# A feed-forward's falling product by Strassen's seven products of quadrants

## What is computed

```python
h2 = rms_norm(x, g_pre_ffn) * (1.0 + sc2) + sh2              # 2048 x 1024, float32
gate, up = jnp.split(h2 @ w_gate_up, 2, axis=-1)             # w_gate_up 1024 x 5632
f = (jax.nn.silu(gate) * up) @ w_down                        # w_down 2816 x 1024
x = x + gt2 * rms_norm(f, g_post_ffn)
```

## Time and profile before

| what | us |
|---|---|
| median of three runs | 3232.58 |
| the profiled execution, its own time | 3233.96 |
| its span, first to last instruction | 3232.2 |
| feed-forward, four chunks of about 364 | 1766 to 3232 |
| in each, rising product | 243 |
| in each, falling product | 120 |

### The profile page before, as it was taken

The page is one execution under the profiler, slowest core; times in us unless marked ns, Lnnn a source line. Parts: engine busy times, 40 slices in busy tenths (PEclk is TensorE's granted clock), DMA queues, the critical chain, the costliest instruction groups (busy, mean ns, idle before and its releaser), DMA issues. The chain is left out here.

```text
span 3232.2 us, 42237 instructions
## 1 busy us (share of the span) xinstructions
PE 2889.3 (89%) x14392; PEld 2338.4 (72%) x14392; DVE 1691.8 (52%) x3092; ACT 1571.3 (49%) x3006; POOL 323.3 (10%) x1001
## 2 busy tenths in 40 slices
PE   6578888788878888689897999999999999999998
PEld 2456666666666667578786888878888788888887
DVE  2246777677868878745454444244433544254433
ACT  0457777778787786875433222232223222232222
POOL 0112222212121120110111000000000000000000
PEclk8787889899989889789998999999999999999999
DMA  5000000000000000121356333343333433343333
GB/s 212 7 24 14 24 14 14 14 14 14 14 4 14 12 27 35 66 102 63 121 175 195 93 97 96 124 144 97 95 123 107 130 97 97 122 144 97 97 98 118
DMA packets 286883, 254.86 MB, mean 79 GB/s; under 512 B 8684, under 2 KB 238616, under 8 KB 286616
## 3 DMA queue, kind: packets, MB, share of 16 engines
q1 hardware_dynamic: 282584, 236.32, 23.6%
q10 hardware_dynamic: 4160, 16.78, 1.4%
HBM read 219.50 MB, written 33.57 MB: 78 GB/s over the span
## 5 line engine op out<-in xcount | busy, mean ns | idle before, releaser
L2104 ACT ACTIVATE p_hi<-raw 128x1024 fp32r<-128x1024 f32 x264 | 279.5, 1059 | 669.4 <-PE ubank L2038 339.0
L2183 DVE TENSOR_TENSOR p_lo<-raw,p_hi 128x1024 fp32r<-128x1024 f32 x264 | 323.5, 1225 | 404.8 <-ACT p_hi L2104 404.8
L1231 ACT ACTIVATE signs<-score,pick 128x512 int8<-128x512 f32 (+6 forms) x224 | 304.8, 1361 | 42.0 <-POOL pick L743 28.5
L1209 ACT ACTIVATE logit<-tbank 128x512 f32<-128x512 f32 (+3 forms) x448 | 215.1, 487 | 211.9 <-PE tbank L962 208.8
L1381 DVE TENSOR_SCALAR_CACHE_REDUCE above<-score,cand 128x384 uint8<-128x384 f32 (+6 forms) x224 | 315.8, 1410 | 3.7
L962 PE MATMUL tbank<-ident,logit 128*128 128x128 f32 x1336 | 249.3, 300 | 69.1 <-ACT logit L1199 61.4
L978 PE MATMUL obank<-vb,logit 128*128 128x64 f32 x2176 | 298.3, 282 | 0.0
L978 PEld LDWEIGHTS obank<-vb,logit 128*128 128x128 f32 x2176 | 292.0, 207 | 0.0
L2036 PE MATMUL gbank<-x_hi,p_hi 128*128 128x512 f32 x704 | 276.5, 393 | 14.8 <-DVE p_lo L2183 14.8
L847 PE MATMUL work<-w_in,h_T 128*128 128x512 f32 (+1 forms) x768 | 283.2, 516 | 0.7 <-ACT h_T L1040 0.7
L2037 PE MATMUL gbank<-keys,p_hi 128*128 128x512 f32 x704 | 275.9, 392 | 0.0
(11 more groups left out here) (236 smaller groups left out, 5143.3 us busy)
## 6 DMA issues: line engine op xcount, KB each, us to landing
raw<-in_w_gate_up SPq DMA_DIRECT2D x176, 512.0 KB, 3.8
raw<-in_w_down SPq DMA_DIRECT2D x88, 512.0 KB, 3.7
w_in<-in_w_ada ACTq DMA_DIRECT2D x4, 4096.0 KB, 13.1
wada<-in_w_ada SPq DMA_DIRECT2D x4, 2048.0 KB, 15.5
row<-in_x SPq DMA_DIRECT2D x16, 512.0 KB, 3.9
mixT<-oT SPq DMA_DIRECT2D x32, 256.0 KB, 2.3
x_rows<-in_x SPq DMA_DIRECT2D x16, 512.0 KB, 4.7
x<-x_rows SPq DMA_DIRECT2D x16, 512.0 KB, 3.1
```

The lines of the kernel that those rows point to most:

```text
L1231: nc.scalar.activation(signs[:, 0:L], score[:, b % 2, 0:L], ACT.Sign, scale=-1.0, bias=pick[:].bitcast(F32), accum_out=less_more[:]).then_ ...
L2104: nc.scalar.activation(p_hi[:, s], raw[:, s], ACT.Copy).then_inc(panel_high, 1)
L2183: nc.vector.tensor_tensor(p_lo[:, s], raw[:, s], p_hi[:, s].bitcast(F32), ALU.subtract).then_inc(panel_ready, 1)
```

## The change

The falling product of a chunk is a product of 512 x 2816 by 2816 x 1024. Both operands are cut into four quadrants: A11 to A22 of 256 tokens by 1408, B11 to B22 of 1408 by 512. Strassen's scheme makes the four quadrants of the result from seven products M1 to M7 in place of eight, each of a sum or difference of quadrants (or a single one) on either side. Each M runs over 11 blocks of 128 rows (KQ). A **unit** is one M at one block: 2 tiles of 128 tokens by 3 matmuls of 128 x 512. There are 77 units in three groups: M1, M2, M5 side by side (units 0 to 32), then M3, M6 (33 to 54), then M4, M7 (55 to 76), each pair or triple turn by turn.

What each engine does for it:

- SyncE loads quadrant blocks of w_down (128 x 512, 256 KB each) into `quads`, four slots of up to three: two quadrants per block in the first group, three in the others. Before, each block of w_down was loaded once per chunk, 11.5 MB; now it is 88 quadrant blocks, 23 MB.
- VectorE makes b_sum (L2306, 512 columns) and a_sum (L2312, 256 columns) for unit u + 3 behind the low parts of unit u, and the low parts of each unit (L2322: 512 columns, into p_lo or b_lo; L2326: 256 columns, a_lo).
- ScalarE makes the high parts of each unit, likewise 512 and 256 columns, in six slots.
- The activations stay unsplit in `a`; the rising step's a_hi and a_lo parts go.
- The seven products are added up in `down`: ScalarE copies M2 and M5 out of their banks, VectorE combines, 16 additions of 512 columns per chunk (L2330): four at unit 35, six at unit 57, six behind the last unit. M4 uses gbank0 and ubank0, so the next rising product waits for its additions.
- The last chunk has no `last_product` any more; its squares follow the last additions.

The diff, cut to its core:

```diff
+KQ = KF // 2
+GROUPS = [("M1", "M2", "M5"), ("M3", "M6"), ("M4", "M7")]
+QUADS = [(11, 22), (12, 22, 11), (21, 11, 22)]
+B_TERMS = {"M1": (11, 22, 1), "M2": (11, None, 0), "M5": (22, None, 0), "M3": (12, 22, -1), "M6": (11, 12, 1),
+           "M4": (21, 11, -1), "M7": (21, 22, 1)}
+A_TERMS = {"M1": (11, 22, 1), "M2": (21, 22, 1), "M5": (11, 12, 1), "M3": (11, None, 0), "M6": (21, 11, -1),
+           "M4": (22, None, 0), "M7": (12, 22, -1)}
+UNITS = [(g, k, m) for g in range(3) for k in range(KQ) for m in GROUPS[g]]
+NU = len(UNITS)
+LOADS = 3 * KQ
...
+
...
-        a_hi = sb("a_hi", [P, KF, TOK], F32R)
-        a_lo = sb("a_lo", [P, KF, TOK], F32R)
+        a = sb("a", [P, KF, TOK])
+        a_hi = sb("a_hi", [P, 6, TOK // 2], F32R)
+        a_lo = sb("a_lo", [P, 6, TOK // 2], F32R)
+        b_hi = sb("b_hi", [P, 2, HALF], F32R)
+        b_lo = sb("b_lo", [P, 2, HALF], F32R)
+        quads = sb("quads", [P, LOAD_SLOTS, 3, HALF])
+        b_sum = sb("b_sum", [P, 3, HALF])
+        a_sum = sb("a_sum", [P, 3, TOK // 2])
...
+        banks = {"M1": dbank[0:2], "M2": dbank[2:4], "M5": (gbank[0], ubank[0]), "M3": (gbank[1], ubank[1]),
+                 "M6": dbank[2:4], "M4": (gbank[0], ubank[0]), "M7": dbank[0:2]}
...
+            def load_quads(c, n):
+                if n >= LOAD_SLOTS:
+                    sp.wait_ge(unit_ready, 2 * (c * NU + last_unit(n - LOAD_SLOTS) + 1))
+                elif not isinstance(c, int) or c > 0:
+                    sp.wait_ge(unit_ready, 2 * c * NU)
+                g, k = divmod(n, KQ)
+                for i, q in enumerate(QUADS[g]):
+                    at = (k + KQ * (q // 10 - 1)) * P
+                    sp.dma_start(quads[:, n % LOAD_SLOTS, i], wd[at:at + P, (q % 10 - 1) * HALF:q % 10 * HALF]
+                                 ).then_inc(quads_in[n % LOAD_SLOTS], 16)
...
+                for n in range(LOAD_SLOTS, LOADS):
+                    load_quads(c, n)
+                    if n == LOAD_SLOTS + 4 and not last:
+
+                        used(sp, c, UP - 1)
+                        load_x(c + 1)
+                    if n == LOAD_SLOTS + 8 and not last:
+                        up_pair(c + 1, 0)
...
+                if refill:
+
+                    pe.wait_ge(vector_drained, c * 16 - (4, 2)[which])
...
+            def unit_product(c, u):
+                g, k, m = UNITS[u]
...
+
...
+                    pe.wait_ge(scalar_drained, c * 4 + 4)
+                bh, bl = b_slot(u, p_hi, b_hi), b_slot(u, p_lo, b_lo)
+                for t in range(2):
+                    ah, al = a_hi[:, u % 6, t * P:(t + 1) * P], a_lo[:, u % 6, t * P:(t + 1) * P]
+                    bank = banks[m][t]
+                    nc.tensor.matmul(bank[:], ah, bh, start=(k == 0), stop=False)
+                    nc.tensor.matmul(bank[:], ah, bl, start=False, stop=False)
+                    mm = nc.tensor.matmul(bank[:], al, bh, start=False, stop=(k == KQ - 1))
+                mm.then_inc(unit_used, 1)
...
+            def unit_high_part(c, u):
+                g, k, m = UNITS[u]
+                if u >= 6:
+
+                    unit_done(act, c, u - 6)
+                elif 1 <= u <= 4:
+
+                    used(act, c, UP - 2 + (u - 1) // 2)
+                if B_TERMS[m][1] is None:
+                    quads_loaded(act, c, u)
+                else:
+                    act.wait_ge(b_summed, c * sums_before(B_TERMS, NU) + sums_before(B_TERMS, u + 1))
+                nc.scalar.activation(b_slot(u, p_hi, b_hi), b_source(u), ACT.Copy).then_inc(unit_high, 1)
+                if A_TERMS[m][1] is not None:
+                    act.wait_ge(a_summed, c * sums_before(A_TERMS, NU) + sums_before(A_TERMS, u + 1))
+                nc.scalar.activation(a_hi[:, u % 6], a_source(u), ACT.Copy).then_inc(unit_high, 1)
...
-                used(act, c, PANELS - 1)
                 for t in range(TPC):
-                    square(dbank[t][:], c, 1, t)
+                    act.wait_ge(vector_drained, c * 16 + (12, 14, 15, 16)[t])
+                    square(down[:, ORDER[t], 0:HALF], c, 1, t)
...
+                for u in range(NU):
+                    unit_high_part(c, u)
+                    if u == 35:
...
+                        act.wait_ge(vector_drained, c * 16 + 10)
+                        for t in range(TPC):
+                            square(down[:, ORDER[t], HALF:], c, 0, t)
+                    if u in (62, 65, 68, 71) and not last:
+                        x_high_part(c + 1, (u - 62) // 3)
...
+                        unit_done(act, c, (NU - 3, NU - 1)[s])
                         panel_high_part(c + 1, 0, s)
...
+            def sums(c, u):
+                g, k, m = UNITS[u]
+                if u >= 3:
+                    dve.wait_ge(unit_ready, 2 * (c * NU + u - 2))
+                first, second, sign = B_TERMS[m]
+                if second is not None:
+                    quads_loaded(dve, c, u)
+                    at = [quads[:, load_of(u) % LOAD_SLOTS, QUADS[g].index(q)] for q in (first, second)]
+                    nc.vector.tensor_tensor(b_sum[:, u % 3], at[0], at[1], ALU.add if sign > 0 else ALU.subtract
+                                            ).then_inc(b_summed, 1)
+                first, second, sign = A_TERMS[m]
+                if second is not None:
+                    if u < len(GROUPS[0]) * KQ:
+                        dve.wait_ge(act_made, c * KF + k + KQ + 3)
+                    nc.vector.tensor_tensor(a_sum[:, u % 3], a_quad(k, first), a_quad(k, second),
+                                            ALU.add if sign > 0 else ALU.subtract).then_inc(a_summed, 1)
+
+            def unit_low_part(c, u):
+                m = UNITS[u][2]
+                dve.wait_ge(unit_high, 2 * (c * NU + u + 1))
+                if B_TERMS[m][1] is None:
+                    quads_loaded(dve, c, u)
+                else:
+                    dve.wait_ge(b_summed, c * sums_before(B_TERMS, NU) + sums_before(B_TERMS, u + 1))
+                nc.vector.tensor_tensor(b_slot(u, p_lo, b_lo), b_source(u), b_slot(u, p_hi, b_hi).bitcast(F32),
+                                        ALU.subtract).then_inc(unit_ready, 1)
+                if A_TERMS[m][1] is not None:
+                    dve.wait_ge(a_summed, c * sums_before(A_TERMS, NU) + sums_before(A_TERMS, u + 1))
+                nc.vector.tensor_tensor(a_lo[:, u % 6], a_source(u), a_hi[:, u % 6].bitcast(F32), ALU.subtract
+                                        ).then_inc(unit_ready, 1)
...
+                unit_done(dve, c, UNITS.index((0, KQ - 1, "M5")))
+                for t in range(2):
+                    dve.wait_ge(scalar_drained, c * 4 + t + 1)
+                    combine(down[:, t + 2, HALF:], banks["M1"][t][:], down[:, t + 2, 0:HALF], ALU.subtract)
...
+                for at, (q, t, m) in enumerate(((12, 0, "M3"), (22, 0, "M3"), (12, 1, "M3"), (22, 1, "M3"),
+                                                (22, 0, "M6"), (22, 1, "M6")), 4):
+                    if m == "M6":
+                        dve.wait_ge(vector_drained, c * 16 + (6, 8)[t])
+                    dst = down[:, t + 2 * (q // 10 - 1), (q % 10 - 1) * HALF:q % 10 * HALF]
+                    combine(dst, dst, banks[m][t][:], ALU.add)
...
+            def drain_third(c, m):
+
+                unit_done(dve, c, UNITS.index((2, KQ - 1, m)))
+                if m == "M7":
+                    for t in range(2):
+                        dve.wait_ge(vector_drained, c * 16 + (11, 13)[t])
+                        combine(down[:, t, 0:HALF], down[:, t, 0:HALF], banks[m][t][:], ALU.add)
+                    return
+                for t in range(2):
+                    for half in range(2):
+                        dst = down[:, t + 2 * half, 0:HALF]
+                        combine(dst, dst, banks[m][t][:], ALU.add)
...
+                    for u in range(3):
+                        sums(c, u)
+                    for u in range(3):
+                        unit_low_part(c, u)
+                        sums(c, u + 3)
...
+                for u in range(3, NU):
+                    unit_low_part(c, u)
+                    if u + 3 < NU:
+                        sums(c, u + 3)
+                    if u == 35:
+                        drain_first(c, first)
+                    if u == 57:
+                        drain_second(c)
+                    if u in (62, 65, 68, 71) and not last:
+                        x_low_part(c + 1, (u - 62) // 3)
+                if last:
+                    gain_half()
+                else:
+                    low_part((c + 1) * UP, 0)
+                drain_third(c, "M4")
                 if not last:
-                    for s in range(2):
-                        low_part((c + 1) * PANELS + s, s)
+                    low_part((c + 1) * UP + 1, 1)
+                drain_third(c, "M7")
```

More of the change, by code:

```diff
@@ L1830, in _, with load_of, last_unit, loaded_count @@
                 tile(NB // 2 - 1, s, s == 0)
+KQ = KF // 2
[8 more added lines that the diff above has]
```

(22 more changed lines are left out.)

255 lines of the change are left out of this document (120 added, 135 removed).

## The result

The changed kernel takes 3336.0 us (median of four runs, 3335.4 to 3336.6), the kernel before 3233.4 on the same chip (3231.3 to 3234.4): ratio 1.032, 95% interval 1.030 to 1.034. It is 3.2% slower. The forecast was 3337 us in a range of 3300 to 3390.

The account below looks back on a forecast made before the run. TensorE bounds the kernel before; VectorE was to bound the falling product after. 3 x 23.4 + 18.8 + 4.8 (turns) + 5.3 (end) + 5 (loop) = 104 us more, giving 3337 us against the median, range 3300 to 3390.

Parts of the forecast that it names:

- VectorE's row of work: Falling product: VectorE becomes the bound, 134.0 us per chunk against 105.1 of matmuls; 4.8 us per triple, 3.7 per pair.
- the self-wait: Falling product: the first sum behind a unit's low parts waits for VectorE's own last instruction, 0.12 us per unit.
- The falling products: Stage on VectorE's clock: 144.1 us against 120.7, so +23.4 per chunk, +18.8 for the last, without x part.
- the loop: Two chunks run in the loop: rows of registers and waits between low parts, 0.03 x 154 = 5 us.
- The edges: Three turns to the next chunk: TensorE starts 1.1 us late, a stall grows 0.5; 4.8 us in all.
- The stall before step 1: Next rising product: TensorE's 2.0 us stall before step 1's gate grows by about 0.5, as squares begin later.
- The tail: Kernel's end: 14.4 us behind the last matmul's slot against 9.1, so +5.3; roots 1.9 apart.
- VectorE keeping up: Rival, falling product: VectorE has units ready every 1.365 us, so the kernel gets faster, 3183 us; chance 0.03.
- Full durations: Rival, falling product: VectorE operations cost their own durations, self-wait nothing; +12.8 us per chunk, 3388 us; chance 0.04.
- late weights: Rival, falling product: weight loads come too late at 142 GB/s; +32 us per chunk, 3465 us; chance 0.04.
- The clock did fall in the gaps: Rival, falling product: TensorE's pauses drop its clock to 1.2 GHz, 210 us per chunk, 3600 us; chance 0.05.
- TensorE's waits: Sign, falling product: TensorE waits 27 to 39 us per chunk, matmuls' modelled ends filling 0.16 of each gap.

## Why the prediction came out right

**VectorE's row of work** was the step on which all hung, and it holds by rows: 4.80 us per triple (4.8 forecast), 3.67 per pair (3.7), 0.11 for the self-wait (0.12). An eighth of the loads left the stage as it was, a third fewer matmuls shortened it by 1.2 us, and taking the weight sums from VectorE by 29.

**The falling products**: 3 x 23.4 + 18.8, with 5 for the loop, were 94 us; they measured 89.5. Chunk 0 grew by 22.1 instead of 23.4 and the last by 17.6 instead of 18.8. The working behind the forecast had 4.82 us a triple and 3.68 a pair; they took 4.79 and 3.66, which makes 0.8 of the 1.3, and the self-wait was counted 77 times where 74 units have one, 0.4 more. The loop's chunks cost 2.8 each over chunk 0, where I took 2.5. I had ascribed that to rows of registers between the low parts, spread evenly; it stands in 23 places behind a self-wait, and removing the self-wait removed it.

**The edges**: 4.8 us for three turns measured 6.7 (4.5 of pauses and 2.2 in the rising products). The late start was priced at 1.1 and took 1.4 to 1.7. The stall before step 1 was to grow by 0.5 and grew by 0.28, 0.88 and 0.25, and the rising products by 0.4, 1.0 and 0.7. So each turn was underpriced by 0.6.

**The tail** is the term that was mis-sized: +5.3 forecast, +7.1 measured. Its other steps came about as worked out: first square 3.6 behind the last low part (3.8), first root 2.2 later (2.1), 5.1 from the last root to the end (5.1). Only the roots were 2.6 apart on average ((3328.87 - 3321.15) / 3) and not 1.9, which makes the 2 us. The rows say where this comes from. Before, VectorE's first pass of a tile reads the bank itself (out_rows from dbank, L2249), and GpSimd's two small operations lie beside it at 0.19 us each; only the third (1.06) meets the passes that read SBUF alone. After the change the sums lie in SBUF, so the first pass, too, has two inputs there (out_rows from down and row, L2403), and GpSimd's multiplication and addition meet such a pass as well. While VectorE still adds from banks, at 3320.05, they take 0.19 as before. That the input from the bank makes the difference was not tried by itself. The errors of falling products (-4.5) and of edges and tail (+3.7) nearly cancel, and 1.6 us of earlier start makes up the rest. So part of the closeness of 3336 to 3337 is luck.

**The rivals.** VectorE keeping up would have shown 4.1 per triple. Full durations fell with the four buffers, late weights with the small loads. The clock did fall in the gaps, but little; stretches of the change behind the emptying of banks, and one well before them (columns as above):

```profile
2052.80:2060.00 7.20, 6.84 (x29) 4.68 (x27) 7.06 (x16) 4.39 (x10) 0.00 (x0) 1.00 0.95 309
2060.00:2067.00 7.00, 3.57 (x14) 2.10 (x12) 6.86 (x15) 5.21 (x12) 0.00 (x0) 0.92 0.71 210
2067.00:2074.00 7.00, 5.78 (x16) 4.62 (x17) 6.90 (x14) 2.50 (x6) 0.00 (x0) 0.59 0.47 143
2110.00:2117.00 7.00, 3.07 (x8) 2.27 (x8) 6.76 (x13) 3.71 (x11) 0.00 (x0) 0.76 0.32 104
```

Pauses of some 0.5 us in every unit left it at 1.00; only behind the two long ones, where TensorE idled 4.3 and 3.9 us while VectorE emptied banks, do the means lie between the two levels (0.59 is mostly 1.2 GHz). VectorE is busy over 96% of those stretches too, so the slower matmuls hid behind it. The forecast of a clock of 1.00 throughout was wrong, without a price.

**TensorE's waits** were forecast at 27 to 39 us per chunk, and its idle time in chunk 0's stage is 22 (144.1 less 121.9). By spacing the matmuls left 37.7 us free (142.8 less 105.1), as forecast; but the first matmul behind a pause is drawn 0.48 us long on average and the others 0.39, and so fills more of the gap than the 0.16 I took off.

## What to carry to other kernels

A change that saves on the engine that bounds must be priced on the engine that feeds it: write down the feeder's work per unit, by spacing from start to start, and compare it with the new, shorter unit. Where an algebraic saving needs sums of operands that don't change, make them once where the feeder has slack; here that, with the fourth buffer, turned 3.2% slower into 0.9% faster. And look at what a buffer's wait really waits for: with three buffers it was the instruction just issued, and a fourth bought 37 us.

## What the runs showed of the hardware beyond what was expected

- VectorE's operations with two inputs in SBUF and GpSimd's nearly exclude each other: one of 512 columns took 1.78 us beside GpSimd and 0.69 alone, one of 256 columns 1.51 and 0.41. An idle GpSimd is no free adder.
- The same holds for small things: GpSimd's multiplication and addition on one column a partition took 0.19 us beside VectorE's passes that read a bank of PSUM, and 0.6 to 1.2 beside those that read SBUF alone. By these rows, moving the result from banks to SBUF ahead of the last passes cost the end of the kernel 2 us.
- A wait for the engine's own last instruction cost VectorE 0.11 us (0.45 instead of 0.34 from start to start), and in a loop, where the count is computed in registers, 0.21 in 22 places of a chunk: 11.4 instead of 8.8 us per chunk.
- Busy times averaged over a stage can hide that its bound changes within it. Without the weight sums the stage took 113.3 us for 108.2 of TensorE and 106.4 of VectorE. VectorE's 1.40 us per unit gave it no lead in the first group, and the first emptying of banks cost 3.7 us; in the run with the sums made once it took 1.27 per unit, and the same place cost 0.3.
